# Norms over heads with their sums in one row per head, spread by wide matmuls, and roots from the reciprocal square root

## What is computed

```python
def rms_norm(x, g):
    y = xf * lax.rsqrt(jnp.mean(xf * xf, axis=-1, keepdims=True) + EPS)
    return (y * g.astype(jnp.float32)).astype(x.dtype)
...
def layer_norm(x, g, b):
    mu = jnp.mean(xf, axis=-1, keepdims=True)
    xc = xf - mu
    var = jnp.mean(xc * xc, axis=-1, keepdims=True)
    y = xc * lax.rsqrt(var + EPS) * g.astype(jnp.float32) + b.astype(jnp.float32)
...
def l2_norm(x):
    return x * lax.rsqrt(jnp.sum(x * x, axis=-1, keepdims=True) + EPS)
```

## Time and profile before

| | us |
|---|---|
| median of 3 runs | 1508.98 (1508.48 to 1509.87) |
| profiled execution, its own time | 1509.2 |
| span of its instructions | 1507.0 |
| PE busy | 1401.1 (93%) |
| DVE busy | 353.7 (23%) |
| ACT busy | 178.6 (12%) |

### The profile page before, as it was taken

The page is one execution under the profiler, slowest core; times in us unless marked ns, Lnnn a source line. Parts: engine busy times, 40 slices in busy tenths (PEclk is TensorE's granted clock), DMA queues, the critical chain, the costliest instruction groups (busy, mean ns, idle before and its releaser), DMA issues.

```text
span 1507.0 us, 15701 instructions
## 1 busy us (share of the span) xinstructions
PE 1401.1 (93%) x6182; PEld 655.4 (43%) x6183; DVE 353.7 (23%) x935; ACT 178.6 (12%) x348; POOL 36.6 (2%) x44
## 2 busy tenths in 40 slices
PE   6997998998989999999998999999999999999886
PEld 4775776896444333333332333333333333332222
DVE  2496626333551101111010101100110011001002
ACT  2011252210010100001000001000001000000002
POOL 3101001000000000000000000000000000000000
PEclk9999997987966999999999999999999999999998
DMA  9648212014455999999980999999999999999925
GB/s 251 139 139 88 84 56 57 1 57 141 170 217 204 416 416 418 417 417 414 418 358 2 414 415 416 418 416 416 416 418 417 415 415 417 418 415 415 414 105 214
DMA packets 86364, 446.52 MB, mean 296 GB/s; under 512 B 9456, under 2 KB 10368, under 8 KB 53360
## 3 DMA queue, kind: packets, MB, share of 16 engines
q1 hardware_dynamic: 82960, 436.45, 73.8%
q0 software_dynamic: 2720, 7.13, 1.9%
q10 hardware_dynamic: 576, 1.37, 0.3%
HBM read 440.53 MB, written 4.39 MB: 295 GB/s over the span
## 4 chain that ended last, share of the span: by engine, by line
PE 72%; DMA 21%; DVE 3%; issue 2%; SPq 1%; ACT 1%; ACTq 0%; DVEq 0%
PE ps L1048 21%; DMA arena<-in_w_gate_up 17%; PE ps L1076 10%; PE ps L711 10%; PE ps L1027 6%; PE ps L1086 3%; PE ps L929 2%; PE ps L1041 2%; DMA arena<-in_w_down 1%; DMA arena<-in_w_main 1%; SPq L359 1%; PE ps L922 1%; PE ps L816 1%; PE ps L750 1%; PE ps L1127 1%
## 5 line engine op out<-in xcount | busy, mean ns | idle before, releaser
L1048 PE MATMUL ps<-arena 128*64 128x512 f32 x2048 | 460.0, 602 | 13.1 <-DMA arena<-in_w_gate_up 12.9
L1048 PEld LDWEIGHTS ps<-arena 128*64 128x64 f32 x2048 | 145.6, 138 | 326.2 <-issue 277.9
L1076 PE MATMUL ps<-arena 128*64 128x512 f32 x1024 | 227.3, 595 | 10.1 <-issue 6.8
L1590 DVE TENSOR_SCALAR arena<-ps 128x512 f32<-128x512 f32 x32 | 22.1, 692 | 726.4 <-PE ps L1048 726.4
L711 PE MATMUL ps<-arena 128*128 128x320 f32 x576 | 161.8, 444 | 14.2 <-DMA arena<-in_w_main 8.5
L1076 PEld LDWEIGHTS ps<-arena 128*64 128x64 f32 x1024 | 82.8, 137 | 132.4 <-issue 127.1
L711 PEld LDWEIGHTS ps<-arena 128*128 128x128 f32 x576 | 112.4, 196 | 63.3 <-issue 19.3
L1027 PE MATMUL ps<-arena 128*128 128x256 f32 (+1 forms) x384 | 121.7, 447 | 0.0
L1027 PEld LDWEIGHTS ps<-arena 128*128 128x128 f32 (+1 forms) x384 | 67.8, 204 | 66.3 <-issue 61.9
L1086 PE MATMUL ps<-arena 128*128 128x512 f32 (+1 forms) x192 | 79.4, 617 | 1.3 <-ACT arena L619 1.3
L608 ACT ACTIVATE arena<-ps 128x512 f32<-128x512 f32 x32 | 19.1, 597 | 478.7 <-PE ps L1048 478.7
(11 more groups left out here) (288 smaller groups left out, 920.1 us busy)
## 6 DMA issues: line engine op xcount, KB each, us to landing
arena<-in_w_gate_up SPq DMA_DIRECT2D x256, 1024.0 KB, 20.2
arena<-in_w_down SPq DMA_DIRECT2D x128, 1024.0 KB, 23.8
arena<-in_w_main SPq DMA_DIRECT2D x40, 512.0 KB, 3.6
arena<-in_w_merge_out SPq DMA_DIRECT2D x1, 3072.0 KB, 10.5
arena<-in_w_conv_out POOLq DMA_DIRECT2D x1, 2048.0 KB, 13.1
arena<-in_w_delta_out SPq DMA_DIRECT2D x1, 2048.0 KB, 9.0
out_delta_s<-arena POOLq DMA_DIRECT2D x1, 2048.0 KB, 15.1
arena<-in_xT SPq DMA_DIRECT2D x1, 1280.0 KB, 6.6
```

What stands on the lines that cost most here:

```text
L1048: m = pe.matmul(ps[SLOTS * (q % 2):SLOTS * (q % 2 + 1), q // 2, :], tokens[:, k], w[:, q * 512:(q + 1) * 512], start=False, stop=(k == KD ...
L1076: m = pe.matmul(ps[SLOTS * c:SLOTS * (c + 1), 2, :], actT[:, r, a * SLOTS:(a + 1) * SLOTS], pieces[UPS + r][:, a, c * 512:(c + 1) * 512], ...
L1590: ts(upb, ps[:, 1, :], 1.0 + LIMIT, 1.0 - LIMIT, ALU.min, ALU.max).then_inc(chain, 1)
```

## The change

- `head_squares`: for each head one matmul with the squares (128 x 320) as the moving operand and, as the stationary one, a window of `pick_qk` or `pick_o`, a block of zeros with one column of ones, so that head h's sums come out in row h: 8 rows of 320 numbers for q and k, 4 for the output. `pick_o` has 1/128 for one.
- `spread_heads`: for each head one matmul, with column h of the identity (8 or 4 rows) broadcast to 128 columns as the stationary operand, and the rows of roots (8 or 4 x 320) as the moving one.
- Roots: the scale moves into the block of ones (`unit`, `unit_c`) or into the Square activation; DVE only adds EPS; ACT gives the reciprocal square root; the reciprocal on DVE is gone; the Newton step stays.
- The layer norm's mean is read by the subtraction straight from PSUM.
- Five more memsets run on GpSimd (POOL), PE's first matmul waits for them, ACT waits for `x_norm_mm` before the first root and no longer behind it, and PE waits for `s_p_done` before the second spread.

```diff
         def _(pool):
-            pool.memset(unit, 1.0).then_inc(sem("zeros"), 1)
+            pool.memset(unit, 1.0 / D).then_inc(sem("zeros"), 1)
+            pool.memset(unit_c, 1.0 / (CC * P)).then_inc(sem("zeros"), 1)
+            pool.memset(pick_qk, 0.0).then_inc(sem("zeros"), 1)
+            pool.memset(pick_o, 0.0).then_inc(sem("zeros"), 1)
+            pool.wait_ge(sem("zeros"), 4)
+            pool.memset(pick_qk[:, 2 * H - 1:2 * H], 1.0).then_inc(sem("zeros"), 1)
+            pool.memset(pick_o[:, H - 1:H], 1.0 / P).then_inc(sem("zeros"), 1)
...
             def root(y, v, count):
                 act.wait_ge(sem("root_in"), count)
-                act.activation(y, v, ACT.Sqrt).then_inc(sem("root_out"), 1)
+                act.activation(y, v, ACT.Abs_reciprocal_sqrt).then_inc(sem("root_out"), 1)
...
+            act.wait_ge(sem("x_norm_mm"), 1)
             root(rb_y, rb, 1)
-
-            act.wait_ge(sem("x_norm_mm"), 1)
...
-            root(head_y, head_ss, 3)
+            root(head_r[0:2 * H], rb[0:2 * H], 3)
...
-            root(head_y, head_ss, 4)
+            root(head_r[0:H], rb[0:H], 4)
...
-                act.activation(yout[0:n, t], xs[0:n, t], ACT.Square,
+                act.activation(yout[0:n, t], xs[0:n, t], ACT.Square, scale=D ** -0.5,
...
-            def head_squares(count, squares, bank, done):
-
-                for t in range(NT):
-                    for h in range(count):
-                        c = 2 * H * t + h
-                        i = pe.matmul(ps[0:TILES[t][1], bank, c:c + 1], squares[:, h, tok(t)], ones[:, 0:1],
-                                      start=True, stop=True)
+            def head_squares(count, squares, picks, bank, done):
+
+                for h in range(count):
+                    i = pe.matmul(ps[0:count, bank, 0:N], picks[:, count - 1 - h:2 * count - 1 - h], squares[:, h],
+                                  start=(h == 0), stop=(h == count - 1))
                 i.then_inc(done, 1)
 
-            def spread_heads(first, end, done):
+            def spread_heads(count, first, end, done):
 
                 for h in range(first, end):
-                    for t in range(NT):
-                        n = TILES[t][1]
-                        i = pe.matmul(ps[:, h, tok(t)], over(head_y[0:n, t, h:h + 1], n, P), cid[0:n, 0:n],
-                                      start=True, stop=True)
+                    i = pe.matmul(ps[:, h, 0:N], over(cid[0:count, h:h + 1], count, P), head_r[0:count],
+                                  start=True, stop=True)
                 i.then_inc(done, 1)
 
-
-            pe.wait_ge(sem("zeros"), 1)
+            pe.wait_ge(sem("zeros"), 6)
...
-            head_squares(H, osq, 4, sem("on_mm"))
+            head_squares(H, osq, pick_o, 4, sem("on_mm"))
             pe.wait_ge(sem("head_root"), 2)
-            spread_heads(0, H, sem("on_mm"))
+            pe.wait_ge(sem("s_p_done"), 2)
+            spread_heads(H, 0, H, sem("on_mm"))
...
-            def root(y, v, temp, count):
-
+            def root(y, v, v_eps, temp, count):
+
+                ts(v_eps, v, EPS, None, ALU.add).then_inc(sem("root_in"), 1)
                 dve.wait_ge(sem("root_out"), count)
-                link(dve.reciprocal(y, y))
                 link(tt(temp, y, y, ALU.mult))
-                link(stt(out=temp, in0=temp, scalar=-0.5, in1=v, op0=ALU.mult, op1=ALU.mult))
-                link(stt(out=y, in0=temp, scalar=1.5, in1=y, op0=ALU.add, op1=ALU.mult))
...
+                link(stt(out=temp, in0=temp, scalar=-0.5, in1=v_eps, op0=ALU.mult, op1=ALU.mult))
+                return stt(out=y, in0=temp, scalar=1.5, in1=y, op0=ALU.add, op1=ALU.mult)
...
             dve.wait_ge(sem("c_sum_mm"), 1)
-            link(ts(rb, ps[:, 4, 0:N], 1.0 / (CC * P), None, ALU.mult))
-            tt(cacc, cacc, over(rb.unsqueeze(1), P, CC, N), ALU.subtract).then_inc(sem("c_centred"), 1)
+            tt(cacc, cacc, over(ps[:, 4, 0:N].unsqueeze(1), P, CC, N), ALU.subtract).then_inc(sem("c_centred"), 1)
...
-            head_sums(H, 4, 1.0 / P)
-            root(head_y, head_ss, head_t, 4)
-            dve.memset(rb, 0.0).then_inc(sem("head_root"), 1)
+            root(head_r[0:H], ps[0:H, 4, 0:N], rb[0:H], rb_t[0:H], 4).then_inc(sem("head_root"), 1)
```

More of the change, by code:

```diff
@@ L233, in hybrid_step @@
         rb, rb_y, rb_t = early(N), early(N), early(N)
-        head_ss, head_y, head_t = early(NT, 2 * H), early(NT, 2 * H), early(NT, 2 * H)
+        head_r = early(N)
+        unit_c, pick_qk, pick_o = early(P), early(4 * H - 1), early(2 * H - 1)
         s_decay = early(H, NSEQ)
@@ L582, in square_x @@
                     act.wait_ge(sem("x2_ss"), t)
-                act.activation(junk[0:n], xs[0:n, t], ACT.Square,
+                act.activation(junk[0:n], xs[0:n, t], ACT.Square, scale=D ** -0.5,
                                accum_out=stat[0:n, t:t + 1]).then_inc(sem("x2_ss"), 1)
@@ L733, in _ @@
             for j in range(CC):
-                i = pe.matmul(ps[:, 4, 0:N], ones, cacc[:, j], start=(j == 0), stop=(j == CC - 1))
+                i = pe.matmul(ps[:, 4, 0:N], unit_c, cacc[:, j], start=(j == 0), stop=(j == CC - 1))
             i.then_inc(sem("c_sum_mm"), 1)
@@ L738, in _ @@
             for j in range(CC):
-                i = pe.matmul(ps[:, 5, 0:N], ones, csq[:, j], start=(j == 0), stop=(j == CC - 1))
+                i = pe.matmul(ps[:, 5, 0:N], unit_c, csq[:, j], start=(j == 0), stop=(j == CC - 1))
             i.then_inc(sem("c_sum_mm"), 1)
@@ L1236, in _ @@
             tt, ts, stt, cp = dve.tensor_tensor, dve.tensor_scalar, dve.scalar_tensor_tensor, dve.tensor_copy
-            def root(y, v, temp, count):
+            def root(y, v, v_eps, temp, count):
+                ts(v_eps, v, EPS, None, ALU.add).then_inc(sem("root_in"), 1)
                 dve.wait_ge(sem("root_out"), count)
-                link(dve.reciprocal(y, y))
                 link(tt(temp, y, y, ALU.mult))
-                link(stt(out=temp, in0=temp, scalar=-0.5, in1=v, op0=ALU.mult, op1=ALU.mult))
-                link(stt(out=y, in0=temp, scalar=1.5, in1=y, op0=ALU.add, op1=ALU.mult))
-            def head_sums(n, bank, scale):
-                for r, t in ((P, slice(0, 2)), (NS, slice(2, 3))):
-                    src = ps[0:r, bank, 2 * H * t.start:2 * H * t.stop].rearrange("p (t n) -> p t n", n=2 * H)
-                    i = ts(head_ss[0:r, t, 0:n], src[:, :, 0:n], scale, EPS, ALU.mult, ALU.add)
-                    if r == P:
-                        step.done(i)
-                i.then_inc(sem("root_in"), 1)
-            step.done(dve.memset(ab, 0.0))
-            step.done(dve.memset(head_ss, 1.0))
-            step.wait(dve)
+                link(stt(out=temp, in0=temp, scalar=-0.5, in1=v_eps, op0=ALU.mult, op1=ALU.mult))
+                return stt(out=y, in0=temp, scalar=1.5, in1=y, op0=ALU.add, op1=ALU.mult)
+            link(dve.memset(ab, 0.0))
             dve.wait_ge(sem("ld_par"), 16)
             dve.wait_ge(sem("x_norm_mm"), 1)
-            ts(rb, ps[:, 4, 0:N], 1.0 / D, EPS, ALU.mult, ALU.add).then_inc(sem("root_in"), 1)
-            root(rb_y, rb, rb_t, 1)
+            link(root(rb_y, ps[:, 4, 0:N], rb, rb_t, 1))
             for k in range(KD):
@@ L1314, in _ @@
             dve.wait_ge(sem("c_centred"), 1)
-            ts(rb, ps[:, 5, 0:N], 1.0 / (CC * P), EPS, ALU.mult, ALU.add).then_inc(sem("root_in"), 1)
-            root(rb_y, rb, rb_t, 2)
+            link(root(rb_y, ps[:, 5, 0:N], rb, rb_t, 2))
             tt(cacc, cacc, over(rb_y.unsqueeze(1), P, CC, N), ALU.mult).then_inc(sem("c_normed"), 1)
@@ L1329, in _ @@
             dve.wait_ge(sem("qk_mm"), 1)
-            head_sums(2 * H, 4, 1.0)
-            root(head_y, head_ss, head_t, 3)
-            dve.memset(rb, 0.0).then_inc(sem("head_root"), 1)
+            root(head_r[0:2 * H], ps[0:2 * H, 4, 0:N], rb[0:2 * H], rb_t[0:2 * H], 3).then_inc(sem("head_root"), 1)
             dve.wait_ge(sem("ab_mm"), 2)
@@ L1473, in norm @@
                 dve.wait_ge(sem("x2_ss"), t + 1)
-                ts(stat[0:n, col], stat[0:n, col], 1.0 / D, EPS, ALU.mult, ALU.add).then_inc(sem("root_in"), 1)
-                root(stat_y[0:n, col], stat[0:n, col], stat_t[0:n, col], 5 + t)
+                link(root(stat_y[0:n, col], stat[0:n, col], stat[0:n, col], stat_t[0:n, col], 5 + t))
                 if t == 0:
@@ L1683, in final_norm @@
                 dve.wait_ge(sem("x2_ss"), NT + t + 1)
-                ts(stat[0:n, col], stat[0:n, col], 1.0 / D, EPS, ALU.mult, ALU.add).then_inc(sem("root_in"), 1)
-                root(stat_y[0:n, col], stat[0:n, col], stat_t[0:n, col], 8 + t)
+                link(root(stat_y[0:n, col], stat[0:n, col], stat[0:n, col], stat_t[0:n, col], 8 + t))
                 stt(out=yout[0:n, t], in0=xs[0:n, t], scalar=stat_y[0:n, col], in1=fg[0:n],
```

8 lines of the change are left out of this document (4 added, 4 removed).

## The result

| | before | after |
|---|---|---|
| median of 5 runs each, us | 1508.98 (1505.98 to 1509.87) | 1500.12 (1498.92 to 1501.5) |
| profiled execution, its own time, us | 1509.2 | 1501.08 |
| span, us | 1507.0 | 1499.0 |

The ratio is 0.9945, with a 95% interval of 0.9931 to 0.996: 8.9 us faster by the medians, 8.1 between the two profiled executions. The forecast was 12.5 us.

What follows compares the result with a forecast made beforehand. PE was taken to bound the chain up to 828 us, then PE alternating with weights. Terms summed to 11.5 us, 12.5 with the clock: 1509.2 to 1496.7, less 0.2 for the median, 1496.5 us; range 1492.5 to 1501.5.

Steps and rivals of the forecast that it cites:

- the clock's term: At PE's start and the output's heads: less time at half clock, 1.0 us gained together.
- the 1.76 us of the projection behind the squares: PE's projection after the q and k squares: full clock kept, 10.37 us down to 8.61.
- first root, net: First root: reciprocal's 2.19 us goes, a table load of 1.29 us is exposed; 0.90 us gained.
- spread of q and k: Spreading the roots over q and k heads: 16 wide records for 48, 7.83 to 4.31 us, 3.52 gained.
- output: squares, root, spread: Output's heads: squares gain 0.70 us, the root on longer rows loses 0.6, the spread gains 2.86 at half clock.
- layer norm, second norm: Both norms: operations removed from DVE lie under PE's work or a wait for PE; nothing gained.
- final norm: Tail: DVE is the chain through three tiles, each losing a 0.20 us reciprocal step; 0.6 us gained.
- The step that failed first: Front of the kernel: PE holds the chain up to 828 us, so front gains reach the end at full value.
- its third rival: Expert part: its weight stream, not PE, times the first late block, so only the tail counts; 1508.4 us, chance 0.04.
- The rival of the thin matmuls: Head squares and spreads: eight columns or rows count as rest, so the clock falls; 1506.6 us, chance 0.08.
- the rival by which the load costs its length twice: First root: the table load brings as much again, so the root loses 0.4 us; 1497.8 us, chance 0.04.
- The rival of the late block: Expert part: changed router logits give one expert a 65th token and another 32.7 us block; 1529 us, chance 0.02.

Runs made afterwards that it cites:

- experiment 1: Kernel after with ACT's wait for `x_norm_mm` put back behind the first root, so the first table load is hidden: 1501.11 us, ratio 0.9922.
- 6: Kernel before with only the reciprocal square root on ACT in place of root and reciprocal, head helpers unchanged: 1507.81 us, ratio 0.9982.
- 3: Kernel after without the eight small stores of the samples' short convolution state, that output left unwritten: 1488.64 us, ratio 0.9842.
- 4: Kernel before without the same eight small stores of the samples' short convolution state, output left unwritten: 1497.52 us, ratio 0.9906.
- 8: Kernel after with the experts' bias matmuls on 128 rows in place of 32, the added rows zero: 1487.44 us, ratio 0.9849.
- Experiment 2: Kernel after with both spreads on all 128 rows, 120 of them zero: 1495.93 us, ratio 0.9896.
- 10: Kernel after with the two spreads on 32 rows, rows 8 to 31 zero: 1502.67 us, ratio 0.9951.
- 7: Kernel after with square root and reciprocal put back, leaving only the new head helpers: 1510.65 us, ratio 1.0006.
- 5: Kernel after with first table load hidden, spreads on 128 rows, and both convolution states packed into stores of long rows: 1477.12 us, ratio 0.9782.
- 9: Kernel after with first table load hidden, spreads on 128 rows, packed convolution-state stores, and bias matmuls on 128 rows: 1463.15 us, ratio 0.969.
- 11: Kernel after with packed convolution-state stores and 128-row spreads, first table load still waiting for `root_in`: 1482.05 us, ratio 0.9812.

## Why the prediction was right, and where it was not

The sign and the size were right: 1500.12 lies inside the range, 3.6 us above the forecast. That it lies inside is in part luck. The range's upper end was made of the clock's term and of the 1.76 us of the projection behind the squares. Of these only the first failed, and the 2.9 us that were lost besides, 0.9 ahead of the layer norm and 2.0 behind the spread, had no place in it. Every part that the forecast priced by a row came out near it where it stands:

| term | forecast, us | measured in the chain, us |
|---|---|---|
| first root, net | 0.90 | 0.84 at PE's start (5.63 less 4.79); nothing of it at the layer norm's sum |
| squares of q and k | 1.73 | 1.83 |
| projection behind them | 1.76 | 1.56 |
| spread of q and k | 3.52 | 3.32 |
| output: squares, root, spread | 0.70, -0.60, 2.86 | 0.57, -0.59, 2.83 |
| layer norm, second norm | 0 | 0: no new lead behind them |
| final norm | 0.60 | 0.6 |
| clock, at the start and the output | 1.0 | start: 0 (5.8 us at half before, 6.0 after); output projection: 0.3 (20.07 and 19.78); behind the first spread: 2.0 lost |

**The step that failed first** is "whatever is taken off the chain in the front moves the block, the stream behind it and the end by as much, and I carry front gains to the end at full value". It holds from the heads on: the 7.64 us of lead at the output are 7.38 to 8.09 at the places of the table in the expert part. It doesn't hold ahead of the layer norm. There the projection has a weight stream of its own, and it is late behind the small stores. PE waits 8.55 us in the kernel before and 9.39 after, its records take 0.7 more, partly at half clock behind the waits, and of the 1.55 us 0.02 are left. Experiments 1 and 6 show gains of 1.23 and 2.55 us shrink to 0.3 and 0.48; in experiments 3 and 4, without the stores, a lead of 1.27 us at PE's start is not lost. The forecast asked this very question of the expert part only (its third rival) and not of the projection, whose wait stood in the same chain behind the earlier trace rows, at 118.54.

**The second step** is the clock's term, "I take 1.0, here and at the output's heads together". At the start it brought nothing: PE began earlier and the clock came back earlier by as much, and behind the first spread it cost 2.0 us. The rival of the thin matmuls had the mechanism half right. With eight columns of weights the clock stayed up, which the forecast had from L760's form; with eight rows it fell, for which it had found no row. The loss behind the spread, 2.0 us, is close to the 1.7 that the rival gave to the delta rule's first matmuls. But in the kernel after the spread itself was done before the clock fell (4.51 us, not 6.0; it took 6.38 and 6.14 in experiments 3 and 8), and the squares kept it, so the rival's 1506.6 was far off. Experiment 2 shows it by the rows alone, and 8 in another stage; 10 shows a smaller loss with 32 rows.

The account: 12.47 forecast, before rounding; less 0.9 of the root, which was lost up to the layer norm's sum; less 1.0 of clock, of which only 0.3 came, and that was gone again at the first `up`; less 0.45 by which the priced pieces at the heads and the output came out smaller together; less 2.0 behind the spread. That gives 8.1, as between the profiled executions; between the medians it is 8.9.

**The table load.** It took its 1.28 us on the path and hardly more: from the end of PE's sums to the projection are 4.79 us, and 3.44 in experiment 1, where it is hidden. The Trainium skill's page "ScalarE: Activation LUTs", section "What ACT_TABLE_LOAD costs", counts a drain of 1.38 us as well; by that figure DVE's step at 16.66 would have stood near 18.0. No run here shows such a drain; ACT had nothing under way when the load began. So the rival by which the load costs its length twice is out. The rival of the late block did not come: the leads in front of and behind the first `down` of a late block lie within 0.7 us of each other, where a block more would take 32.7.

**What stays open.** The weights of the projection's last wait land at 140 to 142.7 us in the executions of before, after, 1, 2, 6, 7 and 8, whose projections start between 17.72 and 21.99, and at 144.87 in 10. Why so little of the start is left in the landing is argued from the stores' share of the engines; shown is only what their removal and their packing do. How long the clock stays at half at PE's start differs between executions of the same instructions there (0 and 3.4 us in 5 and 9; 3.2 to 6.0 in after, 2, 3, 8, 10 and 11), and no experiment changed that alone. The swing of up to 3.7 us in the expert part, on which experiment 7's loss rests for nearly half, has no shown cause.

## What to carry to other kernels

A gain is worth what the next wait lets through: after the place that is made faster, follow the chain to the next transfer it meets, in the same stage too, and ask whether that transfer starts earlier. When a matmul with few rows is put in, look at the clock of what runs behind it and not only at its own length; zeros up to 128 rows cost no time, and here gave back 4.6 us where 2.0 were missed. Many small stores with rows of some bytes are worth packing first, even if nobody waits for the store itself, for the loads beside them may be waited for. And before one profile is set against another, look how much the same instructions differ between executions: the clock at PE's start alone was worth up to 1.7 us between two executions of one front here.

## What was not expected of the hardware

- 16 records of 320 columns with 8 rows in use, 4.5 us without a gap, are followed by half clock for about 10 us; in two of five profiles it began inside the 16 records and lasted 17 us. With 32 rows it began inside them and lasted 6.8; with 128 rows the clock stays at 1.00 for the next 18 us. With 8 columns and 128 rows, 8.7 us (L761 and L690) stay at 1.00.
- 12 records with 32 rows left the clock at half, and 48 matmul records with 128 rows behind them, 25.2 us without a pause, did not bring it back. With 128 rows in those 12, it was back within the stretch from 435 to 440 us (0.80).
- Eight stores of 18 KB in rows of 12 bytes brought what the DMA engines moved down to 63 GB/s at 0.86 busy, and one 512 KB block took 23.2 us, where the median is 3.6; packed with the convolution's, they took the waits away and the layer norm's sum came 16.2 us earlier, with experiments 1 and 2 in; part of it is the clock at the projection's start.
- The first root's table load: 1.28 us, 0.01 to the activation, no drain.
